# Six of twelve modulation tiles multiplied and summed by VectorE in PSUM in place of the matrix engine

## What is computed

```python
cond = jax.nn.silu(c)                      # c: [1, 1024]
mod = cond @ mod_w[l] + mod_b[l]           # mod_w: [1024, 6 * 1024]
shift1, scale1, gate1, shift2, scale2, gate2 = jnp.split(mod, N_MOD, axis=-1)
h = modulate(rms_norm(x, norm1_g[l]), shift1, scale1)
x = x + gate1[:, None, :] * mixer_sublayer(h, ...)
h = modulate(rms_norm(x, norm2_g[l]), shift2, scale2)
x = x + gate2[:, None, :] * hierarchical_moe(h, ...)
```

## Time and profile before

| what | value |
|---|---|
| time, median of 3 runs | 1045.57 us |
| the runs | 1045.70, 1043.85, 1045.57 us |
| span of the profiled execution | 1040.0 us (its own time is not given beside it) |
| TensorE busy | 964.7 us, 93% |
| VectorE busy | 499.2 us, 48% |
| ScalarE busy | 386.4 us, 37% |
| GpSimd busy | 378.4 us, 36% |
| moved | 252 MB, 242 GB/s over the span |

### The profile page before, as it was taken

How to read it: one execution, slowest core, us unless ns; L and a number is a source line. 1 busy time by engine, 2 the same in 40 slices (tenths; PEclk the granted TensorE clock), 3 DMA queues, 4 the chain that set the end, 5 groups by cost and what they waited for, 6 DMA issues and landing times.

```text
span 1040.0 us, 15136 instructions
## 1 busy us (share of the span) xinstructions
PE 964.7 (93%) x6089; PEld 715.1 (69%) x6089; DVE 499.2 (48%) x857; ACT 386.4 (37%) x617; POOL 378.4 (36%) x249
## 2 busy tenths in 40 slices
PE   5999998999999997988797799999999899999997
PEld 2886677776878443343242799877664689999996
DVE  1455258535154631322122506346673358878775
ACT  2633345446333321111020543445650445344442
POOL 0875657435773062554120496760000700000000
PEclk9999999999999999999899899999999999999999
DMA  9996854333579899999998965544104674544421
GB/s 375 338 414 264 353 181 142 102 101 101 164 233 422 352 381 417 412 413 411 404 415 358 389 183 174 174 140 122 41 21 142 221 278 152 218 171 192 187 96 40
DMA packets 49706, 252.07 MB, mean 242 GB/s; under 512 B 10480, under 2 KB 11120, under 8 KB 32240
## 3 DMA queue, kind: packets, MB, share of 16 engines
q1 hardware_dynamic: 43168, 248.09, 63.2%
q0 software_dynamic: 6480, 3.17, 1.1%
HBM read 294.21 MB, written 1.05 MB: 284 GB/s over the span
## 4 chain that ended last, share of the span: by engine, by line
PE 70%; DMA 10%; DVE 8%; issue 6%; POOL 3%; ACT 3%; SPq 0%; DVEq 0%; POOLq 0%; ACTq 0%
PE ps L874 30%; PE ps L1182 17%; DMA tail<-in_experts_dram,xidx 3%; DMA ring<-in_wb_dram 3%; PE ps L1320 2%; PE ps L1396 2%; PE ps L817 2%; PE ps L765 2%; PE ps L1347 2%; PE ps L1335 2%; DMA ring<-in_wa_dram 2%; DMA big<-in_pieces_dram 1%; PE ps L1278 1%; PE ps L1411 1%; DMA xs<-in_x_dram 1%
## 5 line engine op out<-in xcount | busy, mean ns | idle before, releaser
L2216 POOL TENSOR_TENSOR wl<-ring,wh 128x1024 fp32r<-128x1024 f32 (+5 forms) x132 | 287.8, 2199 | 246.8 <-ACT wh L1713 245.4
L1713 ACT ACTIVATE wh<-ring 128x1024 fp32r<-128x1024 f32 (+5 forms) x148 | 144.1, 983 | 175.5 <-PE ps L874 106.7
L874 PE MATMUL ps<-wh,hTh 128*128 128x512 f32 (+4 forms) x400 | 157.3, 393 | 1.2 <-POOL wl L2216 1.1
L874 PE MATMUL ps<-wl,hTh 128*128 128x512 f32 (+4 forms) x400 | 153.2, 383 | 0.0
L874 PE MATMUL ps<-wh,hTl 128*128 128x512 f32 (+4 forms) x368 | 140.2, 381 | 0.0
L1182 PE MATMUL ps<-hTs,wsp 128*128 128x256 f32 x1056 | 128.7, 283 | 0.5 <-DVE wsp L2876 0.5
L1182 PEld LDWEIGHTS ps<-hTs,wsp 128*128 128x128 f32 x1056 | 128.1, 192 | 1.5 <-DVE wsp L2876 0.8
L2204 POOL TENSOR_TENSOR small<-small 128x2 f32<-128x2 f32 (+2 forms) x7 | 5.3, 761 | 275.5 <-DVE small L3180 192.4
L874 PEld LDWEIGHTS ps<-wh,hTh 128*128 128x128 f32 x400 | 75.9, 190 | 23.2 <-issue 8.9
L874 PEld LDWEIGHTS ps<-wl,hTh 128*128 128x128 f32 x400 | 76.2, 191 | 13.3
L874 PEld LDWEIGHTS ps<-wh,hTl 128*128 128x128 f32 x368 | 70.0, 190 | 13.9
(11 more groups left out here) (476 smaller groups left out, 1638.0 us busy)
## 6 DMA issues: line engine op xcount, KB each, us to landing
big<-in_pieces_dram SPq DMA_DIRECT2D x43, 2048.0 KB
ring<-in_wa_dram SPq DMA_DIRECT2D x68, 512.0 KB, 4.0
big<-in_mod_dram SPq DMA_DIRECT2D x11, 2048.0 KB, 10.5
ring<-in_ffn_dram SPq DMA_DIRECT2D x11, 2048.0 KB, 9.1
ring<-in_wb_dram SPq DMA_DIRECT2D x42, 512.0 KB, 3.5
dring<-in_ffn_dram SPq DMA_DIRECT2D x11, 1024.0 KB, 4.9
ring<-in_wb_dram SPq DMA_DIRECT2D x16, 384.0 KB, 4.7
ring<-in_pieces_dram SPq DMA_DIRECT2D x2, 2048.0 KB, 13.0
```

What stands on the lines that cost most here:

```text
L874: mm = pe.matmul(out, x[i], y[j], start=(p, c, k) == (0, 0, 0), stop=(c, k) == (KD - 1, 2), skip_group_check=True)
L1713: nc.scalar.activation(quarter(name, q, "high"), quarter(name, q, "raw"), ACT.Copy).then_inc(s_qh, 1)
L2216: nc.gpsimd.tensor_tensor(quarter(name, q, "low"), quarter(name, q, "raw"), quarter(name, q, "high"), ALU.subtract).then_inc(s_ql, 1)
```

## The change

The last six tiles of the order, 6 to 11, get no row step on TensorE and no copy. In its place VectorE computes, for each, the products of the tile's eight chunks with the eight columns of the conditioning vector (one value per partition), summed in PSUM bank 6; the eighth goes straight to `mpart`. Each product waits for the one before. The sum over the partitions stays as it was. The two slots are freed by `s_mpart` for these tiles in place of `s_gemv`. SyncE's order becomes tile 7, o0, tile 8, o1, tile 9, tile 10, uqr, tile 11 and the rest. TensorE's sums 6 to 9 stand between the halves as the diff shows, sum 10 moves behind o1. VectorE's `mod_columns` now stands behind products 10, and `mod_gate(10)` behind products 11. ScalarE's wait at L1795 goes.

```diff
--- before.py
+++ after.py
@@ -579,7 +579,7 @@
         def used(eng, n):
             eng.wait_ge(*USED[ALL[n][0]])
 
-        NMOD = 12
+        NMOD, BYPE = 12, 6
         MODS = [0, 2, 1, 3] + list(range(4, NMOD))
 
         def mod_slot(j):
@@ -603,7 +603,7 @@
                 n = mod_slot(j)
                 before = [i for i, m in enumerate(MODS[:MODS.index(j)]) if mod_slot(m) == n]
                 if before:
-                    sp.wait_ge(s_gemv, before[-1] + 1)
+                    sp.wait_ge(s_gemv if before[-1] < BYPE else s_mpart, before[-1] + 1)
                 sp.dma_start(mtile[n], mod[j].rearrange("p (c n) -> p c n", c=KD)).then_inc(s_mt[n], 16)
 
             def load(name, stream):
@@ -648,13 +648,14 @@
             mod_tile(6)
             load("v1", wa)
             mod_tile(7)
+            load("o0", wa)
             mod_tile(8)
-            load("o0", wa)
+            load("o1", wa)
             mod_tile(9)
             mod_tile(10)
-            load("o1", wa)
+            load("uqr", wa)
             mod_tile(11)
-            for name, _, _ in LOADS[8:]:
+            for name, _, _ in LOADS[9:]:
                 load(name, wa)
 
 
@@ -907,19 +908,13 @@
             mod_rows(5)
             split_load("v0")
             mod_sum(5)
-            mod_rows(6)
-            split_half("v1", 0)
+            split_load("v1")
             mod_sum(6)
-            mod_rows(7)
-            split_half("v1", 1)
+            split_half("o0", 0)
             mod_sum(7)
-            mod_rows(8)
-            split_half("o0", 0)
+            split_half("o0", 1)
             mod_sum(8)
-            mod_rows(9)
-            split_half("o0", 1)
-            mod_sum(9)
-            mod_rows(10)
+
             def turn_latent(c):
 
                 for t in range(NT):
@@ -929,14 +924,14 @@
                 return mm
 
             split_half("o1", 0)
-            mod_sum(10)
-            mod_rows(11)
+            mod_sum(9)
             pe.wait_ge(s_cn, 2)
             emptied(pe, GI["v3"])
             for c in range(4):
                 mm = turn_latent(c)
             mm.then_inc(s_ctr, 1)
             split_half("o1", 1)
+            mod_sum(10)
             mod_sum(11)
             turn_latent(4)
             for t in range(NT):
@@ -1792,7 +1787,6 @@
                         ins.then_inc(s_cTh, 1)
 
             act.wait_ge(s_ctr, 1)
-            act.wait_ge(s_gemv, NMOD)
             latent_high(0, 4)
             weights_high(LI["uqr"])
             out_gate(2)
@@ -2318,6 +2312,19 @@
                     dve.wait_ge(s_msum, i - 1)
                 V.tensor_copy(mpart[:, i % 2, :], ps[:, 6, :]).then_inc(s_mpart, 1)
 
+            def mod_products(j):
+
+                i, n = MODS.index(j), mod_slot(j)
+                acc = ps[:, 6, :]
+                dve.wait_ge(s_mt[n], 16 * mod_count(j))
+                dve.wait_ge(s_mpart, i)
+                link(V.tensor_scalar(acc, mtile[n][:, 0, :], condw[:, 0, 0:1], None, ALU.mult))
+                for c in range(1, KD - 1):
+                    link(V.scalar_tensor_tensor(acc, mtile[n][:, c, :], condw[:, c, 0:1], acc, ALU.mult, ALU.add))
+                dve.wait_ge(s_msum, i - 1)
+                V.scalar_tensor_tensor(mpart[:, i % 2, :], mtile[n][:, KD - 1, :], condw[:, KD - 1, 0:1], acc, ALU.mult,
+                                       ALU.add).then_inc(s_mpart, 1)
+
             def mod_gate(j):
                 dve.wait_ge(s_msum, j + 1)
                 if j == 4:
@@ -2450,25 +2457,25 @@
             mod_part(5)
             conv(3)
             mod_gate(5)
-            mod_part(6)
-            mod_part(7)
+            mod_products(6)
 
             dve.wait_ge(s_ss, 2)
             link(V.tensor_scalar(small[:, 24:26], small[:, 20:22], 1.0 / QL, EPS, ALU.mult, ALU.add))
             V.tensor_scalar(small[:, 26:28], small[:, 22:24], 1.0 / KVL, EPS, ALU.mult, ALU.add).then_inc(s_ms, 1)
-            mod_part(8)
+            mod_products(7)
             dve.wait_ge(s_rstd, 2)
             for t in range(NT):
                 link(V.tensor_scalar(raw[:, t, 0:QL], raw[:, t, 0:QL], small[:, 24 + t:25 + t], None, ALU.mult))
                 V.tensor_scalar(raw[:, t, 392:RAW], raw[:, t, 392:RAW], small[:, 26 + t:27 + t], None, ALU.mult
                                 ).then_inc(s_cn, 1)
 
-            mod_part(9)
+            mod_products(8)
+            mod_products(9)
+            mod_products(10)
             dve.wait_ge(s_msum, 10)
             mod_columns(1)
-            mod_part(10)
+            mod_products(11)
             mod_gate(10)
-            mod_part(11)
 
             def latent_low(c):
                 if c % 2 == 0:
```

## The result

The changed kernel takes **1048.5 us** (median of 6 runs, 1047.9 to 1051.9), the kernel before 1044.9 us in the same job (6 runs, 1041.5 to 1045.8). The ratio is 1.004, with a 95% interval of 1.0025 to 1.0055: **slower**, by some 3.6 us, where 1.7 us less were forecast. The time lies in the range; the direction was missed, and the case "slower" had been given 0.26.

A forecast was written before the change was run, and what follows sets the result against it. TensorE was taken to bound the stretch before, VectorE its end after. A gain of 3.4 us less 1.7 us for the slow clock gives -1.7 us: span 1040.0 to 1038.3, plus 5.57 around it, 1043.9 us; range 1040.0 to 1049.5.

The forecast's parts named there:

- the case "slower": Whole kernel: slower than before by more than 0.2%, mostly through a dear PSUM write; chance 0.26.
- The price of a product: VectorE's 48 linked operations: 0.78 us each, 6.25 us a tile, 37.5 us for six tiles.
- Rival D: VectorE's products: dear PSUM writes, or first products each waiting 2.4 us for GpSimd, make it slower, up to 1051.6 us; chance 0.27.
- The bound: End of the changed stretch: VectorE's products hold back gate 10, leaving TensorE idle from 130.9 to 137.0 us.
- A: Changed stretch: VectorE bounds and TensorE's clock drops behind its idle time; 1041.8 to 1046.2 us; chance 0.42.
- B: Changed stretch: the clock stays up or slow matmuls hide behind the ropes; -3.4 us, 1042.2 us; chance 0.25.
- The moved loads: SyncE's queue: o0 ahead of tile 8, o1 ahead of tile 9, both land before TensorE asks; no cost.
- Tile 10: VectorE waiting for a transfer: tile 10 takes 7.8 us to land, at 122.7, a stall of 1.6 us.
- The clock: TensorE behind its 6.1 us idle before the last gates: latent's first matmuls run slow, 1.7 us lost.
- the second line of the timetable: VectorE between products 7 and 8: four scalings of the latent rows take 3.7 us again, ending at 108.6.
- signs of being wrong: Wrong if products last 0.69 or 0.9 us, the clock stays 1.00, or TensorE waits at sum 8 or 9.
- the 3.1 us worked out from the page: VectorE's 48 operations: extra cost if a PSUM source took 0.065 us more each, left out of the sum.

The follow-up runs named there:

- experiment 1: Kernel before with only the transfers' new order (o0 ahead of tile 8, o1 ahead of tile 9, uqr ahead of tile 11): ratio to before 1.0015.
- experiment 5: Changed kernel plus unread matmuls on TensorE, 24 ahead of sum 8 and 30 ahead of sum 11: ratio to the kernel before 1.0025.
- experiment 4: Changed kernel plus unread matmuls on TensorE, 24 ahead of sum 8 and 14 ahead of sum 11: ratio to the kernel before 1.0021.
- experiment 6: Changed kernel with the products' running sum in SBUF instead of PSUM bank 6: 1058.2 us, ratio to the kernel before 1.0115.
- 2: Changed kernel with the four scalings of the latent rows on ScalarE instead of VectorE: ratio to the kernel before 1.0014.
- experiment 3: Changed kernel with only tiles 9 to 11 on VectorE, row steps of tiles 6 to 8 back on TensorE: ratio to the kernel before 0.9989.
- 8: Changed kernel with only tiles 6 and 7 on VectorE, 8 to 11 on TensorE, scalings left on VectorE: ratio to the kernel before 0.9982.
- 9: Changed kernel with only tiles 6 and 7 on VectorE and the four scalings on ScalarE: ratio to the kernel before 0.9994.
- 10: Kernel before with only the four scalings moved to ScalarE: ratio to the kernel before 0.9996.
- 7: Changed kernel with only tiles 6 to 8 on VectorE, 9 to 11 on TensorE, scalings on ScalarE: ratio to the kernel before 0.9969.
- 11: Repeat of the kernel with tiles 6 to 8 on VectorE and scalings on ScalarE: median 1041.85 us, ratio to the kernel before 0.9968.

## Why the prediction was wrong

Points that held, with gate 5 as the zero of both axes (the changed trace stands 0.94 us earlier):

- **The price of a product.** Forecast 0.78 us from start to start and 6.25 us a tile; measured 0.79 and 6.3. The operation takes 756 ns. Rival D's dear PSUM write did not come, nor did a product ever wait for GpSimd.
- **The bound.** VectorE sets the end, as in cases A, B and D, from sum 8 on and not only ahead of the last gates.
- **The moved loads** cost nothing (experiment 1). On ScalarE the wait of 8.49 us for o0 was gone; one of 4.50 us for o1 stood in its place at 106.47, and TensorE, whose only two waits are those shown, felt nothing of it.
- **Tile 10**: forecast a landing of 7.8 and a stall of 1.6 us; measured 7.54 and 1.20.
- **The columns**: 1.15 us allowed, 1.05 measured.
- **The clock** fell behind the last wait as forecast. Behind the last transposing matmul, where the sum had 1.7 us for it, it cost 1.3; another 0.8 us went ahead of it, at sum 11, where the sum had nothing (experiment 5). That it fell at sum 8 too was not forecast; it costs nothing (experiment 4).

**The step that failed** is the second line of the timetable: "The four scalings of the latent rows took 3.7 us, of which 2.2 are one wait against GpSimd; GpSimd will be just as busy, so 3.7 again". They took 9.4. On the axis of before, products 7 ended at 104.8 (forecast 104.9), the scalings at 114.2 (forecast 108.6, 5.6 us late), and what follows keeps most of this delay: products 9 at 126.8 (121.1), products 11 at 141.5 (136.35), the last transposing matmul at 145.1 (139.35). Of the 5.75 us there, 5.6 are the scalings; a shorter stall for tile 10 and smaller terms took back 0.5, and from gate 10 to the matmul it took 0.7 longer than forecast, at the lower clock. In the sum: forecast -3.4 + 1.7 = -1.7; measured -3.4 + 5.75 + 1.3 = +3.65. One of the prediction's own signs of being wrong showed this: TensorE waited at sum 8, 5.99 us, where the margin had been put at 0.2.

Both things that lengthened the scalings stood in the prediction's own working. It had the power and the halves of o0 earlier, it had o1's first low quarter ready at 111.6, directly behind o0's four, and it had the scalings at 104.9 instead of 109.7. So the four operations, which had met the tail of GpSimd's work, would now start in its midst, and the pause behind that work was to be filled by o1. I carried the measured sum of four operations over, where three of the four were short only because GpSimd had just stopped: 0.35 to 0.41 us alone, 2.3 to 2.6 us beside it. Rival D named the place next to it ("three or four first products each wait 2.4 us for GpSimd"), priced nearly right, but hung it on the wrong operation: the first product writes PSUM and takes 748 ns whether GpSimd works or not, while one that writes SBUF takes 480 ns alone and 1.88 us once beside GpSimd (experiment 6).

A smaller slip changes nothing in the sum: the 3.1 us worked out from the page count a PSUM source for all 48 operations, but the first of each tile reads none; for the other 42 it is 2.7.

**Shown**, by the stretch more than by the kernels' ratios: the loads (1), the clock's 0 and 2.1 us (4, 5), the scalings' waits as the first of the waits that matter (2, 3), and that the same waits are free where TensorE sets the end (8, 9, 10). **Only argued**: that o1's load alone, left in its old place, would have shortened them. GpSimd would have stopped at 98.69 + 9.42 = 108.1, behind two of the four waits; it wasn't tried, because tile 9 moves with it.

**Open.** The whole-kernel ratio does not order the kernels as the stretch does: experiments 8 and 9 are the shortest in the stretch (73.9 and 73.8 us) and gain 0 to 0.2%, experiments 7 and 11 (74.9 and 75.2) gain 0.3%. Up to the first transfer of the expert stage it took 213.70 us from gate 5 before, 217.6 in the changed kernel (3.9 more, so its loss arrives there), and 209.6, 212.8, 214.2 and 212.6 in experiments 8, 9, 7 and 11, so one trace of each is no measure for gains of this size. What happens to a gain behind the small copy isn't settled.

A measurement's resolution was also put too fine. "About 0.2%" holds for ratios over a dozen runs each; single runs of the kernel before went from 1040.0 to 1048.5 us in 35 of one job. The changed kernel's own 1.004 comes from six runs of each.

## What to carry over

When an operation moves, take its price anew from what its neighbour engine does at the new time: a duration that holds a wait (2.61 us for 0.4 of work) belongs to the moment, not to the operation, and a row of short ones behind it may be short only because the other engine had just stopped. Work that leaves the bounding engine is best given to another one's idle time early in the stretch: two tiles gave their whole 3.7 us, while six stood ahead of the last gates and cost 3.6. And count the next wait before taking out one: with the scalings gone, the tiles' landings took back half.

## What the runs showed of the hardware

- Four scalings from SBUF to SBUF in a row (128 x 384 and 128 x 256) took 2.26 to 2.55 us each beside a GpSimd that worked without a pause in operations of 2.39 us, and 0.35 to 0.41 us each with GpSimd idle: as if GpSimd took its turn between any two of them.
- An operation with scalar, SBUF tile and sum takes the same time with the sum in PSUM (six in 4.71 us) as in SBUF (six in 4.69 us, GpSimd idle). The Trainium skill's page "VectorE: DVE Perf Modes", in its section on the TRN2 errata, charges more for a PSUM source; no row here shows that.
- GpSimd pays as well: beside VectorE operations with two SBUF inputs its quarter went from 2.39 to 2.70 us (experiment 6). Beside the four scalings it stayed at 2.39.
- TensorE's granted clock stood at or near the lower level behind idles of 5.99, 3.79 and 3.28 us, and at 0.66 and 0.68 in the stretches around idles of 1.64 and 1.93 us in experiments 7 and 11, ahead of which TensorE had done eight matmuls of one column in 0.95 us. With an idle of 2.02 us behind matmuls of 512 columns, ahead of sum 11 in experiment 3, it stayed at 1.00, as where no gap was longer than 0.79 us (experiment 5). So the length of the idle alone does not tell it; what else does isn't settled here.
